# Moving the expert selections of four tiles to the end of their tile, and re-spacing the background work

## The chip, the cores and the metric

The kernel runs on one core of a Trainium2 chip. The metric is the device time of one execution in microseconds (us). Before the change it is 4654.85 us, the median of three runs from 4640.61 to 4658.42 us.

## The reference, cut to what matters

One decoder layer is computed for a prompt of 1024 positions and for 32 sample positions (8 sequences of 4) that share all weights, in float32 with a width of 1024:

```
h   = rmsnorm(x) * (1 + scale1) + shift1
z   = h @ W_in                                  # q, k, v, gMLP u and v, branch gates
A   = differential attention: 8 heads, two softmax maps each, A1 - lambda * A2 weights the values
B   = u * (tril(W_s) v + b) in chunks of 128
x2  = x + gate1 * (sigmoid(gA) * (A @ W_A) + sigmoid(gB) * (B @ W_B)) @ W_o
h2  = rmsnorm(x2) * (1 + scale2) + shift2
s   = (h2 @ W_q) . subkeys                      # 8 heads, two halves of 128 keys
top 16 of each half, top 16 of their 256 sums -> 8 * 16 = 128 experts for each row, softmax gates
y   = x2 + gate2 * sum over experts e of  g_e * gelu(u_e . h2) * v_e
```

The tables u and v have 16384 rows of 1024 float32 (4 KB) each. Every row of the sequence gathers 128 rows of u and 128 rows of v.

## The kernel before, in words

There are three phases: the conditioning products, the projection to z, and the tail, which holds all the rest and which alone the change touches (`tail_phase`). The rows are cut into nine tiles: tiles 0 to 7 are 128 prompt rows each, tile 8 is the 32 sample rows.

The tail starts with a front part (attention of tiles 0 to 3, the mix of tiles 0 and 1, all of the sample's attention, and the selection of tile 0). Then comes the expert loop, one turn for each tile `t`. In turn `t`:

- POOL issues indirect gathers in turn: one brings, for one of the 128 expert slots, a u row for each of the 128 rows of tile `t` (`u_rows`, line 971), the next brings the 128 v rows of one row of tile `t-1` (`v_rows`, line 981). One gather moves 128 rows of 4 KB, or 512 KB. Eight u buffers and eight v buffers are in flight; a gather waits until its buffer was used.
- DVE makes, in program order, one `dot` (line 1877) for each u gather, which waits for that gather. A turn has 128 of them. I call the place of a dot its **slot** `s` (0 to 127). Four slots are a **tick**; a turn has 32 ticks, and the ticks are numbered through: turn 1 begins at tick 32.
- PE adds four v gathers to the result of tile `t-1` in each tick (`add_rows`, line 1307).
- After a dot DVE may do pieces of two other kinds of work. One is the **selection** of tile `t+1`: 81 steps (`select`) that search the scores (MAX8, MATCH_REPLACE8, FIND_INDEX8), build the expert numbers and the gates. The other is the **background**.

The background is a written timetable, `BACK`. It holds the mixes of the pairs of tiles (2,3), (4,5), (6,7) and of the sample (`mix` 1 to 4, 35 steps each: the branch products, x2, h2, and the scores of the selection) and the attention of tiles 4 to 7 (`att` 1, 39 steps). Each entry has steps, a first tick and an end tick, and `timetable` spreads the steps evenly over the ticks; where there are more steps than ticks, two steps share a tick. SP (loads and stores), PE, ACT and DVE each run their part of a step at its tick in their own program order; DVE spreads a step over the four slots of the tick. A mix loads 20 weight blocks of 1 MB through SP's queue: three at its step 0, with the rows of its tiles, one at each of its steps 7 to 14 and 17 to 20, and one at each of its steps 25 to 29, with its part of the sub-keys. In the second entry all attention steps stand ahead of those of mix 2.

A selection can start when the mix that makes its scores is done. There are two places for it. A tile `t` that is not in `LATE` runs the selection of tile `t+1` from slot 36 on, one step after each dot; SP loads its scores at tick 8 of the turn and the h2 rows of the next tile at tick 2. A tile in `LATE` runs it from slot 84 on, two steps after each dot, with the loads at ticks 20 and 21:

```
if t < PT and t not in LATE and S0 <= s < S0 + STEPS:        # S0 = 36, STEPS = 81
    select(t + 1, s - S0)
if t in LATE and S1 <= s:                                    # S1 = 84
    for i in range(2 * (s - S1), min(2 * (s - S1) + 2, STEPS)):
        select(t + 1, i)
for kind, p, k, quarter in AT_SLOT.get(t * P + s, ()) if t < PT else ():
    background[kind](p, k, quarter)
```

ACT's exponential of the gates (`gate_exp`) stands at tick 25, or 29 in a late tile. The first u gather of the next turn waits on POOL for the selection's expert numbers (`s_idx`). After turn 7 the sample's numbers and gates are packed, and its gathers follow.

Of the kernel before, what the change touches and what calls it, by code (L numbers as in the profile page):

```python
# [481 lines left out]
def att_steps(p):  # L482
    return H * len(GROUPS_ATT[p]) + 7
# [6 lines left out]
def every(kind, p):  # L490
    n = {"att": lambda: att_steps(p), "mix": lambda: MIX_STEPS, "satt": lambda: SATT_STEPS}[kind]()
    return [(kind, p, k) for k in range(n)]


def spread(steps, others):

    out, n = [], 0
    for i, step in enumerate(steps):
        out.append(step)
        while n < len(others) and n * len(steps) < (i + 1) * len(others):  # L500
            out.append(others[n])
            n += 1
    return out


def timetable(parts):

    ticks, slots = {}, {}
    for steps, begin, end in parts:
        for i, step in enumerate(steps):  # L510
            ticks.setdefault(begin + i * (end - begin) // len(steps), []).append(step)
    for tick, steps in ticks.items():
        for n in range(TICK * len(steps)):
            slots.setdefault(TICK * tick + n // len(steps), []).append(steps[n // TICK] + (n % TICK,))
    return ticks, slots


def tail_phase(nc, g):
# [22 lines left out]
    KR = 4  # L541
    TPT = P // TICK
    FRONT = spread(every("att", 0) + every("mix", 0), every("satt", 0))
    BACK = ((every("mix", 1), 0, 35),
            (every("att", 1) + every("mix", 2), 35, 116),
            (every("mix", 3), 116, 168),
            (every("mix", 4), 168, 232))
    LATE = (3,)
    AT_TICK, AT_SLOT = timetable(BACK)
    GSTEP = [6, 7, 8, 9, 10, 11, 12, 13, 16, 17, 18, 19] + list(range(24, 32))  # L550

# [44 lines left out]
    place, main, last_in = {}, 0, {}  # L596
    for step in FRONT + [step for steps, _, _ in BACK for step in steps]:
        for key in units(*step):
# [44 lines left out]
    with ExitStack() as ctx:  # L643
# [125 lines left out]
        with nc.Block() as block:  # L769
            @block.sync  # L770
            def _(sp):
# [132 lines left out]
                def load_scores(f):  # L904
                    for b in range(2):
                        sp.wait_ge(s_sst[b], 16 * 4 * min(2 * (f // 2 + 1), TILES))
                    if f > 0:
                        sp.wait_ge(s_idx, f)
                    sp.dma_start(q[0:rows(f), :], g.sc[f * P:f * P + rows(f), :]).then_inc(s_scl, 16)
# [18 lines left out]
                def next_x2(d):  # L928
                    sp.wait_ge(s_st, 16 * (d + 1))
                    if d + 1 < PT:  # L930
                        sp.dma_start(xy[:], g.x2[(d + 1) * P:(d + 2) * P, :]).then_inc(s_x, 16)
                    if d + 1 == PT:
                        for j in range(GP4):
                            m = NS // GP4
                            sp.dma_start(xy[32 * j:32 * j + m, :], g.x2[NP + j * m:NP + (j + 1) * m, :]).then_inc(s_x, 16)
                            for n in range(2):
                                r = 32 * j + n * NDEC
                                sp.dma_start(g2[r:r + NDEC, :],
                                             g.mod[1 + 2 * j + n:2 + 2 * j + n, cols].broadcast_to([NDEC, D])).then_inc(s_g2, 16)
                for t in range(TILES):  # L940
                    for tick in range(TPT if t < PT else 0):
                        for kind, p, k in AT_TICK.get(t * TPT + tick, ()):
                            background[kind](p, k)
                        if tick == (21 if t in LATE else 2) and 1 <= t < PT:
                            sp.wait_ge(s_u, U0[t])
# [3 lines left out]
                        if tick == 6 and t >= 2:  # L949
                            next_x2(t - 2)  # L950
                        if tick == (20 if t in LATE else 8):
                            load_scores(t + 1)
# [373 lines left out]
            def _(act):  # L1326
# [120 lines left out]
                def gate_exp(f):  # L1447
                    r = rows(f)
                    act.wait_ge(s_df, f + 1)
                    nc.scalar.activation(best[0:r], best[0:r], ACT.Exp).then_inc(s_ex, 1)  # L1450

                def gelu(t, c):
                    cols = slice(c * CH, (c + 1) * CH)
                    act.wait_ge(s_u, U0[t] + (c + 1) * CH)
                    nc.scalar.activation(ge[:, cols], a[:, cols], ACT.Gelu).then_inc(s_ge, 1)  # L1455
# [24 lines left out]
                for t in range(TILES + 1):  # L1480
                    for tick in range(TPT):
                        if t in LATE and tick == 29:
                            gate_exp(t + 1)
# [8 lines left out]
                        if t == PT and tick in (18, 31):  # L1492
                            gelu(t, (18, 31).index(tick))
                        if t < PT and t not in LATE and tick == 25:
                            gate_exp(t + 1)

            @block.vector
            def _(dve):
# [344 lines left out]
                def select(f, i):  # L1843

                    if i < 38:
                        (halves_even, halves_odd)[i % 2](f, i // 2)
                    elif i < 40:
                        candidates(f, i - 38)
                    elif i < 62:
                        (sums_even, sums_odd)[i % 2](f, (i - 40) // 2)  # L1850
                    elif i == 62:
                        difference(f)
                    elif i < 65:
                        places(f, i - 63)
                    elif i < 77:
                        pick(f, i - 65)
                    elif i < 79:
                        experts(f, i - 77)
                    elif i < 81:
                        gates(f, i - 79)  # L1860
# [19 lines left out]
                def weights(t, c):  # L1880
                    cols = slice(c * CH, (c + 1) * CH)
                    dve.wait_ge(s_ge, W0[t] + c + 1)
                    if c == 0 and t > 0:
                        dve.wait_ge(s_wt, t)
                    gt = gate[:, t % 2, cols] if t < PT else gate_s[:, cols]
                    if c == 0:
                        dve.wait_ge(s_gate if t < PT else s_pk, t + 1 if t < PT else 2 * QS)
                    nc.vector.tensor_tensor(w[:, cols], ge[:, cols], gt, ALU.mult).then_inc(s_w, 1)
# [19 lines left out]
                for t in range(TILES + 1):  # L1908
                    if t == PT:
                        pack_sample()  # L1910
                    for s in range(NU[t] if t <= PT else 0):
# [5 lines left out]
                        if s % CH == 8 and s > CH:  # L1917
                            weights(t, s // CH - 1)
                        if t < PT and t not in LATE and S0 <= s < S0 + STEPS:
                            select(t + 1, s - S0)  # L1920
                        if t in LATE and S1 <= s:
                            for i in range(2 * (s - S1), min(2 * (s - S1) + 2, STEPS)):
# [13 lines left out]
def build(nc, ins, outs):  # L1936
    g = Shared()
    with ExitStack() as ctx:
# [63 lines left out]
        run(adaln_phase)  # L2002
        run(projection_phase)
        run(tail_phase)


# [61 lines left out]
```

## Time and profile before

| what | value |
|---|---|
| median of three runs | 4654.85 us |
| the profiled execution's own time | 4671.97 us |
| its span, first to last instruction | 4670.3 us |
| busy: PE, DVE, POOL, ACT | 63%, 55%, 57%, 13% |
| DMA | 1550 MB, mean 332 GB/s |
| begin of the expert loop (first dot) | 1497.0 us |
| start of the last dot | 4608.6 us |

The busy shares are means over phases with different limits; the expert loop has to be read by stretches. The rows below cut a turn at slots 0, 36, 84 and 128, which are the places where the selections begin. I call the three stretches the first, middle and last third of a turn, though they have 36, 48 and 44 slots.

### The profile page before, as it was taken

The numbers are of one execution on the slowest core, as the hardware profiler recorded it, in microseconds if no ns is written. First come the engines' busy times: TensorE is split into PE (matmuls) and PEld (weight loads), VectorE is DVE, ScalarE is ACT, GpSimd is POOL, SyncE is SP. The second block draws the span as 40 slices with busy tenths as digits, with TensorE's granted clock in tenths as the row PEclk, the third lists the DMA queues.
The fourth block names the chain that finished last, engine by engine and source line by source line (L and its number), as shares of the span: only waits on it lengthen the run. The fifth ranks groups of instructions, "written<-read, shape, count | busy, mean of one in ns | idle before, by whom it ended". The sixth has DMA issues, their size and how long they took to land.

```text
span 4670.3 us, 46877 instructions
## 1 busy us (share of the span) xinstructions
PE 2941.9 (63%) x16545; PEld 1779.0 (38%) x16545; DVE 2569.1 (55%) x5693; ACT 586.4 (13%) x1207; POOL 2670.9 (57%) x2513
## 2 busy tenths in 40 slices
PE   2899999896882675877365644555534344633354
PEld 1677777564772562434143322322301112300010
DVE  2466633333115896997675448467467556556411
ACT  1111133322111012333000100000000000000000
POOL 2223222233322567877676668667677777777776
PEclk7899999877986786788687776777767665565666
DMA  7322321789974999999999999999999999999999
GB/s 270 123 98 95 125 78 62 251 304 349 351 268 178 368 377 411 383 366 394 419 407 420 419 417 361 408 418 418 412 383 416 405 415 390 400 414 380 352 412 358
DMA packets 468719, 1550.14 MB, mean 332 GB/s; under 512 B 51638, under 2 KB 108407, under 8 KB 453084
## 3 DMA queue, kind: packets, MB, share of 16 engines
q0 software_dynamic: 351376, 1271.99, 69.3%
q1 hardware_dynamic: 116268, 262.92, 14.8%
q10 hardware_dynamic: 864, 12.58, 0.7%
q8 instruction: 113, 1.85, 0.2%
q14 instruction: 98, 0.80, 0.0%
HBM read 1482.18 MB, written 65.23 MB: 331 GB/s over the span
## 4 chain that ended last, share of the span: by engine, by line
POOL 32%; DMA 19%; PE 14%; issue 11%; DVE 5%; POOLq 1%; ACT 0%; SPq 0%; DVEq 0%; ACTq 0%
POOL v_rows L981 16%; POOL u_rows L971 15%; DMA v_rows<-in_peer_v,expertsT 14%; PE ps_y L1307 5%; DMA u_rows<-in_peer_u,experts 3%; PE ps_bank L1166 2%; DVE u_rows L1877 2%; DMA v_rows<-in_cache_v 2%; PE ps_bank L1160 2%; PE ps_bank L1084 1%; PE ps_y L1265 1%; PE ps_bank L1087 1%; POOL u_rows L981 1%; PE ps_y L1224 1%; DMA u_rows<-in_peer_v,expertsT 0%
## 5 line engine op out<-in xcount | busy, mean ns | idle before, releaser
L1877 DVE CUSTOM_DVE_ANT_0 u_rows<-u_rows,h_rows 128x1024 f32<-128x1024 f32 x1056 | 1292.7, 1225 | 1075.5 <-DMA u_rows<-in_peer_u,experts 903.6
L1307 PE MATMUL ps_y<-v_rows,w_columns 128*32 128x512 f32 x4016 | 806.6, 944 | 1310.2 <-DMA v_rows<-in_peer_v,expertsT 1275.4
L971 POOL DMA_INDIRECT u_rows<-in_peer_u,experts x1024 | 1114.0, 1088 | 448.4 <-issue 296.3
L981 POOL DMA_INDIRECT v_rows<-in_peer_v,expertsT x1004 | 1090.9, 1087 | 466.2 <-issue 280.2
L1307 PEld LDWEIGHTS ps_y<-v_rows,w_columns 128*32 128x32 f32 x4016 | 161.7, 147 | 1812.2 <-issue 1810.6
L374 PE MATMUL ps_z<-w_in_high,hT_high 128*128 128x512 f32 (+1 forms) x1008 | 398.9, 396 | 1.5 <-ACTq L383 1.5
L374 PE MATMUL ps_z<-w_in_high,hT_low 128*128 128x512 f32 (+1 forms) x1008 | 397.5, 394 | 0.0
L374 PE MATMUL ps_z<-w_in_low,hT_high 128*128 128x512 f32 (+1 forms) x1008 | 396.1, 393 | 0.0
L349 POOL CAST w_in_high<-w_in_buf 128x4096 fp32r<-128x4096 f32 x13 | 46.8, 3602 | 456.8 <-PE ps_z L374 427.5
L1166 PE MATMUL ps_bank<-turned_a,weights 128*128 128x256 f32 (+1 forms) x1280 | 282.6, 383 | 0.9 <-ACT turned_a L1330 0.9
L1160 PE MATMUL ps_bank<-weights,turned_a 128*128 128x256 f32 (+1 forms) x1152 | 268.9, 394 | 1.8 <-ACT turned_a L1330 1.8
L1166 PEld LDWEIGHTS ps_bank<-turned_a,weights 128*128 128x128 f32 x1280 | 243.8, 213 | 59.7 <-issue 32.9
L1160 PEld LDWEIGHTS ps_bank<-weights,turned_a 128*128 128x128 f32 (+1 forms) x1152 | 215.6, 189 | 75.9 <-issue 37.7
L423 DVE TENSOR_TENSOR z_square<-z_raw 128x512 f32<-128x512 f32 (+1 forms) x54 | 82.4, 1525 | 240.2 <-ACT z_raw L390 235.6
L374 PEld LDWEIGHTS ps_z<-w_in_low,hT_high 128*128 128x128 f32 (+1 forms) x1008 | 181.3, 180 | 53.3
L374 PEld LDWEIGHTS ps_z<-w_in_high,hT_low 128*128 128x128 f32 (+1 forms) x1008 | 180.8, 179 | 54.1
L374 PEld LDWEIGHTS ps_z<-w_in_high,hT_high 128*128 128x128 f32 (+1 forms) x1008 | 180.7, 179 | 53.6 <-ACTq L383 1.7
L1455 ACT ACTIVATE gelu_now<-a_now 128x16 f32<-128x16 f32 x66 | 14.2, 215 | 1352.1 <-DVE a_now L1877 1351.9
L1084 PE MATMUL ps_bank<-kT,qT 64*128 64x512 f32 (+3 forms) x384 | 181.0, 582 | 4.2 <-DVE att_rows L1555 2.5
L1002 POOL DMA_DIRECT2D v_rows<-in_cache_v x128 | 67.9, 531 | 191.9 <-issue 191.0
L995 POOL DMA_DIRECT2D u_rows<-in_cache_kT x128 | 68.2, 532 | 168.9 <-issue 165.9
L1362 ACT ACTIVATE prob<-ps_bank,exp_bias 128x512 f32<-128x512 f32 (+2 forms) x192 | 110.4, 578 | 301.9 <-DVE exp_bias L1523 217.9
(244 smaller groups left out, 3626.8 us busy)
## 6 DMA issues: line engine op xcount, KB each, us to landing
u_rows<-in_cache_kT POOLq DMA_DIRECT2D x128, 512.0 KB, 5.8
v_rows<-in_cache_v POOLq DMA_DIRECT2D x128, 512.0 KB, 6.1
weights<-in_peer_w_q SPq DMA_DIRECT2D x40, 1024.0 KB, 7.7
w_in_buf<-in_w_in POOLq DMA_DIRECT2D x14, 2048.0 KB, 9.4
scratch_z<-z_out SPq DMA_DIRECT2D x112, 256.0 KB, 2.0
weights<-in_w_att_out SPq DMA_DIRECT2D x20, 1024.0 KB, 18.3
weights<-in_w_gm_out SPq DMA_DIRECT2D x20, 1024.0 KB, 8.1
weights<-in_w_out SPq DMA_DIRECT2D x20, 1024.0 KB, 8.1
```

Source lines behind the costliest of these rows:

```text
L374: last = nc.tensor.matmul(ps_z[0:r, n % RING, :], hT[lhs][:, k, t * P:t * P + r], w[rhs][:, b, k, :], start=k == 0 and (lhs, rhs) == (0, 0 ...
L423: link(nc.vector.tensor_tensor(sq[0:r, :], zs[0:r, j, :], zs[0:r, j, :], ALU.mult))
L971: pool.indirect_dma_start(ur[:, slot, :], None, g.peer_u, bass.IndirectOffsetOnAxis(ap=col, axis=0)).then_inc(s_ur[slot], 16)
L981: pool.indirect_dma_start((ur if other else vr)[:, slot, :], None, g.peer_v, bass.IndirectOffsetOnAxis(ap=idxT[:, t % 3, k:k + 1], axis=0) ...
L995: pool.dma_start(skT[:, n % KP, e], g.cache_kT[bass.ds(page, 1)].rearrange("a p h c -> (a p) h c")).then_inc(s_sk[n % KP], 16)
L1002: pool.dma_start(svr[:, n % VP, :], g.cache_vp[bass.ds(page, 1)].rearrange("a p c -> (a p) c")).then_inc(s_svp[n % VP], 16)
L1084: last = nc.tensor.matmul(dst[:, 0:wd], qT[half, par, i * P:(i + 1) * P], kT[half, par, c * CB:c * CB + wd], start=True, stop=not edge)
L1160: last = nc.tensor.matmul(dst[0:r, i * QB:(i + 1) * QB], lT[:, k, i * P:i * P + r], wr[:, slot, k, :], start=k == 0, stop=k == KD - 1)
L1166: last = nc.tensor.matmul(dst[:, jj * QB:jj * QB + n], wr[:, slot, k, jj * P:(jj + 1) * P], A[:, k, 0:n], start=k == 0, stop=k == KD - 1)
L1307: last = nc.tensor.matmul(ps_y[32 * j:32 * (j + 1), b:b + CB], wcol[:, base:base + 32], (ur if four[j][0] else vr)[:, four[j][1], b:b + CB ...
L1362: takes(nc.scalar.activation(prob[:, m, c * CB:c * CB + wd], bank(("s", p, n, m, c))[:, 0:wd], ACT.Exp, bias=nbias[:, b, m:m + 1], scale=S ...
L1877: nc.vector.tensor_tensor_reduce(ur[:, slot, :], ur[:, slot, :], hrow[:, t % 2, :], 1.0, 0.0, ALU.mult, ALU.add, a[:, s:s + 1]).then_inc(s ...
```

## The change

The ticks in the timetable and the set of late tiles change. No instruction is added or removed; the order of the instructions on DVE, PE, ACT and SP does.

```
-    BACK = ((every("mix", 1), 0, 35),
-            (every("att", 1) + every("mix", 2), 35, 116),
-            (every("mix", 3), 116, 168),
-            (every("mix", 4), 168, 232))
-    LATE = (3,)
+    BACK = ((every("mix", 1), 0, 52),
+            (every("att", 1) + every("mix", 2), 52, 116),
+            (every("mix", 3), 116, 180),
+            (every("mix", 4), 180, 244))
+    LATE = (1, 3, 5, 7)
```

In ticks per step: mix 1 goes from 1.00 to 1.49, attention and mix 2 (74 steps) from 1.09 to 0.86, mix 3 from 1.49 to 1.83; mix 4 stays at 1.83 and begins 12 ticks later. Tick 52 is slot 80 of turn 1, tick 116 slot 80 of turn 3, tick 180 slot 80 of turn 5 and tick 244 slot 80 of turn 7.

## Rows read from the trace of the kernel before

**Rows 1.** The page, the span in 40 slices: DMA busy, GB/s.
```profile
DMA  7322321789974999999999999999999999999999
GB/s 270 123 98 95 125 78 62 251 304 349 351 268 178 368 377 411 383 366 394 419 407 420 419 417 361 408 418 418 412 383 416 405 415 390 400 414 380 352 412 358
```

**Rows 2.** The page, chain that ended last, by engine.
```profile
POOL 32%; DMA 19%; PE 14%; issue 11%; DVE 5%; POOLq 1%; ACT 0%; SPq 0%; DVEq 0%; ACTq 0%
```

**Rows 3.** Turns 0, 1, 2, by thirds: us, PE PEld DVE ACT POOL busy, PEclk, DMA share, GB/s.
```profile
1496.96:1569.31 72.35, 40.49 (x179) 34.70 (x178) 55.58 (x102) 6.77 (x13) 49.31 (x40) 0.74 0.95 354
1569.31:1668.52 99.21, 57.98 (x257) 50.08 (x255) 93.59 (x284) 3.04 (x7) 56.30 (x49) 0.80 1.00 399
1668.52:1754.24 85.72, 68.66 (x337) 60.85 (x337) 82.55 (x167) 19.86 (x33) 57.62 (x43) 0.86 0.95 361
1754.24:1861.53 107.29, 60.94 (x242) 23.91 (x246) 62.81 (x122) 21.96 (x58) 83.35 (x75) 0.68 1.04 411
1861.53:2004.04 142.51, 119.19 (x591) 60.11 (x584) 128.48 (x369) 50.35 (x129) 111.83 (x95) 0.82 1.00 380
2004.04:2136.31 132.27, 103.87 (x518) 53.42 (x517) 119.41 (x271) 44.15 (x117) 103.04 (x88) 0.83 1.00 378
2136.31:2239.66 103.35, 71.22 (x375) 37.03 (x377) 74.09 (x149) 31.92 (x79) 80.41 (x73) 0.83 1.01 396
2239.66:2383.48 143.82, 60.74 (x330) 27.26 (x326) 96.41 (x274) 11.49 (x21) 102.16 (x97) 0.69 1.02 409
2383.48:2523.97 140.49, 95.70 (x467) 59.54 (x458) 88.10 (x184) 5.70 (x10) 97.13 (x91) 0.82 1.02 420
```

**Rows 4.** Turn 3, middle and last third; turn 4, middle; the same columns.
```profile
2632.61:2788.24 155.63, 91.97 (x488) 57.75 (x483) 59.55 (x99) 12.91 (x23) 97.31 (x95) 0.77 1.03 418
2788.24:2926.88 138.64, 67.52 (x349) 34.18 (x341) 116.95 (x338) 9.54 (x17) 111.20 (x91) 0.73 0.96 370
3036.89:3181.52 144.63, 71.06 (x344) 35.12 (x339) 94.35 (x270) 8.25 (x16) 101.97 (x97) 0.68 1.02 417
```

**Rows 5.** Turn 5 and turn 7, by thirds; the same columns.
```profile
3311.32:3418.32 107.00, 43.89 (x224) 20.45 (x227) 46.81 (x78) 6.08 (x12) 73.34 (x70) 0.69 1.03 412
3418.32:3552.82 134.50, 52.94 (x267) 15.24 (x263) 91.50 (x261) 3.42 (x10) 105.28 (x96) 0.66 0.99 384
3552.82:3680.34 127.52, 59.43 (x281) 19.04 (x273) 83.66 (x169) 3.52 (x6) 97.15 (x91) 0.72 1.02 419
4051.01:4148.88 97.87, 37.69 (x176) 13.57 (x179) 47.02 (x77) 1.94 (x8) 72.59 (x72) 0.57 1.02 397
4148.88:4275.00 126.12, 42.90 (x200) 8.25 (x195) 85.32 (x248) 0.87 (x4) 97.41 (x95) 0.62 1.01 397
4275.00:4405.36 130.36, 41.94 (x189) 7.93 (x181) 81.25 (x169) 3.52 (x6) 93.75 (x88) 0.59 0.93 352
```

**Rows 6.** Turn 7 from slot 124 to the first dot of turn 8; the same columns.
```profile
4385.12:4405.36 20.24, 6.39 (x29) 1.10 (x21) 6.07 (x18) 0.22 (x1) 8.02 (x8) 0.58 0.55 200
```

**Rows 7.** DVE groups, turn 1's last third: busy, mean ns, idle before, releaser.
```profile
L1877 DVE CUSTOM_DVE_ANT_0 u_rows<-u_rows,h_rows 128x1024 f32<-128x1024 f32 x44 | 53.6, 1219 | 2.0 <-DMA u_rows<-in_peer_u,experts 2.0
L1546 DVE SCALAR_TENSOR_TENSOR diff_prob<-prob,map_coef 128x1024 f32<-128x1024 f32 (+3 forms) x10 | 10.9, 1090 | 4.8 <-PE ps_bank L1096 4.5
```

**Rows 8.** DVE groups, turn 3's middle third.
```profile
L1877 DVE CUSTOM_DVE_ANT_0 u_rows<-u_rows,h_rows 128x1024 f32<-128x1024 f32 x48 | 58.9, 1227 | 96.0 <-DMA u_rows<-in_peer_u,experts 96.0
```

**Rows 9.** DVE groups, turn 3's last third: mix 3's first and last.
```profile
L1596 DVE SCALAR_TENSOR_TENSOR u_then_b<-ps_bank,gate_bias,u_then_b 128x128 f32<-128x128 f32 x16 | 4.4, 329 | 0.0
...
L1578 DVE RECIPROCAL head_rstd<-head_std 128x8 f32<-128x8 f32 x2 | 0.4, 184 | 0.0
```

**Rows 10.** POOL groups, turn 3's middle third.
```profile
L971 POOL DMA_INDIRECT u_rows<-in_peer_u,experts x48 | 49.1, 1023 | 14.6 <-issue 14.6
```

**Rows 11.** POOL groups, turn 3's last third.
```profile
L971 POOL DMA_INDIRECT u_rows<-in_peer_u,experts x46 | 58.7, 1276 | 14.0 <-issue 14.0
```

**Rows 12.** DMA issues: count, KB each, median us to landing.
```profile
weights<-in_w_att_out SPq DMA_DIRECT2D x20, 1024.0 KB, 18.3
```

## The prediction, made before the change was run

> **What bounds the kernel now.** I read the page's slices first. From slice 14 on the 16 DMA engines are busy over 90% at mostly 360 to 420 GB/s [rows 1], so the expert loop, two thirds of the span, lives by its gathers. The chain of waits agrees: POOL, which issues them, has 32%, DMA 19%, PE 14%, DVE 5% [rows 2]. Then I cut the loop at the slots where selections begin, in the view of windows [rows 3 to 5]. The reader is to see three kinds of stretch. (1) Those at 418 to 420 GB/s with a DMA share over 1.02: the DMA engines are the limit, and DVE waits for u rows (96 of 156 us in turn 3's middle third [rows 8]). I take 418 GB/s as the full rate. (2) Those in which DVE is nearly solid: turn 0's middle and last (93.6 of 99.2, 82.6 of 85.7) and turn 1's (128.5 of 142.5, 119.4 of 132.3), where a dot waits 2 us in all for its row [rows 7] and the rate is 361 to 399. (3) Turn 3's last third, where the kernel already has a late selection: DVE 117 of 139 us, 370 GB/s [rows 4], gathers of 1276 ns each on POOL [rows 11] against 1023 in the third before [rows 10].
>
> Bytes follow as time x rate: turn 3's last third moved 138.64 x 0.370 = 51.3 MB, which at 418 takes 122.7 us. So a late selection loses 16 us in its third. A selection in its ordinary place loses too: turn 5's middle third moved 51.6 MB in 134.5 us where 123.6 would do (11 us), turn 7's 50.1 MB in 126.1 (6 us) [rows 5].
>
> **The change, turn by turn.** No instruction comes or goes, so each turn is what is bound there after the move. A weight block is 1.05 MB [rows 12]; with its other loads and stores I count 34 MB for a prompt mix, 22 for the sample's, 1.6 for a head of attention. Against 418 GB/s, 1 MB is 2.4 us.
>
> *Turn 0.* Mix 1 had 32 of its steps here, now 22 (the last is step 21): 9.6 MB leave, and on DVE little (the h2 pair, some 5 us). DVE was busy 55.6 + 93.6 + 82.6 = 231.7 of 257.3 us [rows 3]. If DVE becomes the only limit, 231.7 - 5 and a first load of about 9 us leave 236 (-22); if the 25.6 us of waits stay, -4. The waits lie mostly in the first third, whose loads at mix step 0 don't move. I take -14.
>
> *Turn 1, slots 0 to 84.* The selection goes and attention goes, mix 1's steps 22 to 34 come. Before, 107.3 x 0.411 + 142.5 x 0.380 = 98.3 MB in 249.8 us. Now 84 pairs of gathers (88.1) + 10.1 of mix 1 + 2.6 of the first two heads + 0.5 = 101.3 MB, DVE nearly free: 242 us at 418. -8 (0 if the rate stays where it is, -15 if fewer loads fall before slot 84).
>
> *Turn 1, slots 84 to 128.* Here the whole selection (two steps a slot) meets attention, now at 1.16 steps a tick where it was 0.91. Selection and 44 dots cost what turn 3's last third shows without mix 3: 117 less 13.8 (six DVE groups, the first and last in [rows 9]) = 103 us. An attention step costs DVE between 3.8 and 5.2 us: the third held ten of them before, as its ten rows of L1546 show [rows 7], and the same third of turn 7, which has none, was busy 81.3 us; 119.4 - 81.3 gives 3.8 of work, 132.3 - 81.3 gives 5.1 with waits for PE (middle third: (142.5 - 85.3)/11 = 5.2). Now steps 2 to 13 run here, 11 full ones: 42 to 57 us. Sum 145 to 160, against 132.3 before. DVE has no slack in this third, so I am nearer the upper end: 160, +28 (bounds +13 and +33, the latter with 12 full steps).
>
> *Turn 2.* Attention's last step is at slots 80 to 83 instead of 48 to 51. DVE in the first third 74 + 2.4 steps x 3.8 = 83 of 103 us, in the middle 96 - 11 (mix 2's beginning goes) + 12 x 3.8 = 131 of 144: it fits, but only just. Bytes -0.9 MB. I take +3 (-5 to +20; the upper end is rival D's).
>
> *Turns 3, 4, 6: bytes alone.* Mix 2 brings 5.8 MB more into turn 3 ahead of slot 84, at 418 (+14), mix 3 2 MB less behind it, where DVE is the limit (-1). Turn 4 loses 4.9 MB at 417 (-12), turn 6 gets 1.5 (+4). Together +5 (-5 to +10).
>
> *Turn 5.* Slots 0 to 84: 95.7 MB before; mix 3's end brings 7.0, mix 4's beginning is as large as before, the loads at ticks 2 and 8 (1.5 MB) go behind slot 84. 101 MB at 418 is 242 us, against 241.5: the selection's 11 us pay for the bytes. Last third: like turn 3's, with a mix half as large: 130, against 127.5. +3. Bounds: -12 if the late third runs at 418 (47.4 MB, 113 us), +11 if it is turn 3's 138.6.
>
> *Turn 7.* The same way: 89 + 5.9 - 1.5 = 93.4 MB, 223 us against 224. Last third: 130.4 before, of which 20 us are the drain behind slot 124, when POOL has no numbers for the sample's rows yet [rows 6]. Now 125.6 (turn 3's slots 84 to 124) - 13 + 20 + 3 for a selection that ends seven slots later: 136. +6 (-9 to +14).
>
> *Waits.* POOL's first u gather of the next turn waits for the expert numbers, which come after dot 123 instead of 114; queued behind it are v gathers, and PE waits for those. By then POOL has seven u rows issued ahead, and turn 3 shows this end already: it is in its 138.6. SP's score load moves from tick 8 to 20, one tick ahead of its reader as now, behind the q, k and v loads of two heads in turn 1.
>
> Sum: -14 - 8 + 28 + 3 + 5 + 3 + 6 = **+23 us**. The profiled execution took 4671.97 (span 4670.3 and 1.7 around it): 4695. That execution lies 17 above the median of the runs, 4654.85; a difference carries over, so 4678.
>
> On what dense DVE work does to the gathers: the row is POOL's 1276 ns a gather in the late third against 1023 [rows 10, 11]. The Trainium skill (SBUF — State Buffer, section "Who interferes with whom") says that only copies, casts and scalar operations in their two-port modes keep GpSimd from writing descriptors, and that searches, reductions and two-tensor operations don't; the selection is nearly all of the latter. By that rule the late third would run at the full rate; this trace has it at 370, with the cause open. The rule would put turns 5 and 7 at their lower ends; its result is rival B.
>
> **The rivals.** *B: it comes out even.* The late third is slow in turn 3 by accident of its place, DVE's 105 us lie beside gathers at 418, and turns 5 and 7 give -12 and -9 instead of +3 and +6: +23 - 30 = -7, and with turn 1's third at 150, not 160, it is -17 at the least. For it: DVE has 20 us to spare in that third [rows 4]. Against: POOL is without a pause there, and its gathers are longer. Time 4648 (4638, or 4663 if of the two only turn 5 gains).
>
> *C: faster.* One mechanism: DVE's work, not the bytes, costs the rate. Then every stretch that loses its selection runs at 418 and turn 0 gains all its waits: -22 - 15, and the jam in turn 1 costs only the work, +13, because the waits for PE (5 us in ten steps [rows 7]) vanish in longer ticks; turns 5 and 7 -12 and -9, the rest +8: -37, 4618. It decides from the point where turn 1's last third stays under 145 us and turn 5's middle third reaches 418. Against: DVE was without slack in that third already.
>
> *D: clearly slower.* Attention at 1.16 steps a tick fills PE. In turn 1's middle third PE was busy 119.2 of 142.5 us for 11 steps; turn 7's, with the additions alone, 42.9. So a step costs 6.9 us and a tick's additions 3.6; 6.9 x 1.16 + 3.6 + the idle time as it was (1.9) = 13.5 us a tick, where it was 11.9: over 21 ticks of turn 2 +34, less my 3: +54, 4709. Against: the granted clock (a mean over its two levels, 1.2 and 2.4 GHz) was 0.82 to 0.86 of 2.4 GHz in the stretches in which PE was busiest, 0.57 to 0.69 in idle ones [rows 3, 5], so a fuller PE is a faster one.
>
> That the timetable binds nothing is excluded: DVE and PE run their steps in program order between the dots and the additions.
>
> **How the numbers follow.** A measurement tells some 0.5% (23 us) from no change. Chances: forecast 0.42, B 0.26, C 0.16, D 0.16. The forecast's own bounds (-10 to +50, not all ends at once) put half of it above +23 and the rest within. Slower: 0.21 + 0.16 + a little = 0.40; same: 0.20 + 0.22 = 0.42; faster: C and the low end of B, 0.18. The likeliest case gives 4678; range 4630 to 4728, which cuts off half of C and the far end of D. The likeliest case alone: 4645 to 4705.
>
> **What would show it.** Right: turn 0 near 243 us; turn 1's slots 84 to 128 at 155 to 165 with DVE solid and POOL waiting for DVE's dots, which it doesn't do there now; the first two thirds of turns 1, 5 and 7 at 410 GB/s or more; late thirds of turns 5 and 7 under 390. Wrong: turn 1's last third under 145 or turn 2 over 400 with PE solid; gathers of the late thirds near 1023 ns.

## The result, and the profile after

The changed kernel takes 4722.06 us (median of five, 4713.91 to 4724.69), against 4654.85: a ratio of 1.0153, 95% interval 1.0134 to 1.0171. It is slower by 67 us; the forecast was +23. The profiled execution took 4724.01 us with a span of 4722.2.

First the page of the changed kernel: two lines of the span in 40 slices, and the chain that ended last by engine (they answer to [rows 1, 2]).

```profile
DMA  7323221789866999999999999999999999999899
GB/s 278 114 95 112 107 75 64 258 328 371 335 228 234 364 356 418 412 328 351 365 397 420 419 418 353 418 419 403 406 413 372 388 408 411 363 417 410 324 420 359
...
POOL 29%; DMA 20%; PE 14%; issue 11%; DVE 8%; POOLq 1%; ACT 0%; SPq 0%; DVEq 0%; ACTq 0%
```

The largest falls against [rows 1] are in slices 18 to 20 (turn 1's late third and most of turn 2's first two: 328, 351 and 365 for 366, 394 and 419), in 31 and 38, which hold the late thirds of turns 5 and 7 (372 and 324 for 416 and 352), and in 35, the end of turn 6 (363 for 400). Slice 25, turn 3's late third, has 353 and was low before too (361). DVE's share of the chain grew from 5% to 8%.

Next the windows of the changed kernel, cut at the same slots as [rows 3 to 5] and with the same columns: turns 0, 1 and 2 by thirds, turn 3's middle and last third, turn 4's middle, turns 5 and 7 by thirds.

```profile
1483.77:1554.02 70.25, 33.81 (x151) 29.13 (x152) 53.92 (x98) 7.09 (x13) 52.68 (x40) 0.71 0.95 355
1554.02:1647.51 93.49, 34.58 (x139) 28.82 (x137) 89.11 (x275) 0.65 (x3) 64.84 (x50) 0.69 0.95 359
1647.51:1735.88 88.37, 32.01 (x145) 27.69 (x145) 86.13 (x183) 11.26 (x18) 53.66 (x43) 0.67 0.90 331
1735.88:1839.97 104.09, 59.01 (x294) 34.87 (x295) 45.65 (x76) 6.16 (x14) 75.66 (x73) 0.73 1.02 413
1839.97:1980.69 140.72, 76.24 (x398) 40.70 (x400) 61.48 (x105) 11.49 (x25) 104.73 (x99) 0.73 1.03 414
1980.69:2140.62 159.93, 128.67 (x554) 65.49 (x547) 152.72 (x438) 48.82 (x133) 101.03 (x87) 0.78 0.89 326
2140.62:2254.97 114.35, 99.82 (x521) 56.29 (x523) 92.41 (x199) 51.01 (x130) 81.49 (x74) 0.88 0.99 382
2254.97:2401.97 147.00, 97.97 (x533) 52.39 (x529) 119.13 (x345) 39.00 (x102) 115.71 (x98) 0.82 0.98 369
2401.97:2542.52 140.55, 87.78 (x443) 53.51 (x436) 94.84 (x197) 12.00 (x19) 97.43 (x89) 0.78 1.01 410
...
2662.53:2822.09 159.56, 99.77 (x528) 66.53 (x524) 59.47 (x100) 15.68 (x28) 99.26 (x96) 0.79 1.03 419
2822.09:2961.65 139.56, 54.52 (x287) 22.28 (x280) 116.06 (x334) 9.54 (x17) 111.81 (x91) 0.66 0.95 363
...
3065.10:3205.64 140.54, 75.44 (x384) 40.30 (x376) 92.23 (x268) 3.00 (x8) 99.70 (x99) 0.75 1.03 420
...
3332.59:3443.60 111.01, 58.06 (x297) 35.09 (x301) 46.90 (x77) 5.33 (x12) 80.37 (x74) 0.75 1.02 406
3443.60:3579.97 136.37, 64.17 (x324) 30.12 (x320) 59.50 (x99) 7.40 (x14) 94.93 (x94) 0.70 1.03 412
3579.97:3717.34 137.37, 51.94 (x239) 14.44 (x232) 110.87 (x322) 6.21 (x12) 109.95 (x91) 0.56 0.95 353
...
4093.27:4200.65 107.38, 49.10 (x281) 24.31 (x285) 46.97 (x77) 3.15 (x12) 75.94 (x75) 0.62 1.02 411
4200.65:4326.47 125.82, 63.85 (x311) 29.05 (x305) 59.53 (x99) 3.14 (x12) 94.74 (x95) 0.54 1.03 408
4326.47:4460.42 133.95, 41.65 (x189) 7.84 (x181) 106.64 (x317) 3.52 (x6) 97.97 (x86) 0.61 0.90 341
```

By turns, from first dot to first dot (traces; us):

| turn | before | after | difference | forecast |
|---|---|---|---|---|
| 0 | 257.3 | 252.1 | -5 | -14 |
| 1, slots 0 to 84 | 249.8 | 244.8 | -5 | -8 |
| 1, slots 84 to 128 | 132.3 | 159.9 | +28 | +28 |
| 2 | 387.7 | 401.9 | +14 | +3 |
| 3, 4 and 6 | 402.9, 384.4, 370.7 | 419.1, 370.9, 375.9 | +16, -14, +5 | +13, -12, +4 |
| 5 | 369.0 | 384.8 | +16 | +3 |
| 7 | 354.3 | 367.2 | +13 | +6 |

The loop is 68 us longer by these two traces. Their front parts, which are the same code, differ by 13 us the other way (loop begins at 1497.0 and 1483.8 us). And the trace of before was itself long in turn 7: three other executions of that turn's unchanged code (first_half, denser_att and more_dve_before, below) took 341 us. So turn 7 lost some 26 us, not 13; that trace lay 17 us above the median.

The groups of POOL in the changed kernel, late thirds of turns 1, 3 and 5 in that order; the last columns are the idle time ahead of the group and what ended it (turn 3's pair answers to [rows 11]):

```profile
L981 POOL DMA_INDIRECT v_rows<-in_peer_v,expertsT x43 | 52.6, 1224 | 36.1 <-PE ps_y L1307 25.1 <-issue 11.0
L971 POOL DMA_INDIRECT u_rows<-in_peer_u,experts x44 | 49.5, 1124 | 23.1 <-issue 13.1 <-DVE experts L1829 10.0
...
L981 POOL DMA_INDIRECT v_rows<-in_peer_v,expertsT x45 | 57.4, 1275 | 14.0 <-issue 13.4 <-PE ps_y L1307 0.6
L971 POOL DMA_INDIRECT u_rows<-in_peer_u,experts x46 | 54.7, 1189 | 14.0 <-issue 14.0
...
L971 POOL DMA_INDIRECT u_rows<-in_peer_u,experts x45 | 55.5, 1233 | 13.7 <-issue 13.7
L981 POOL DMA_INDIRECT v_rows<-in_peer_v,expertsT x46 | 54.9, 1194 | 14.0 <-issue 13.7 <-PE ps_y L1307 0.3
```

In turns 3 and 5 POOL has no wait worth naming: its busy time and the pause of 0.30 us behind each gather fill the third (110.0 + 27.4 of 137.4 us in turn 5). POOL is the limit there, because a gather takes 1.2 us instead of 0.95. In turn 1 POOL waits, for PE's additions (25 us) and for the selection's expert numbers (10 us); DVE is busy 152.7 of 159.9 us, so I take it as the limit there.

Why are gathers long? The timeline of the changed kernel, turn 3's last third, shows it: columns are start, duration, engine, line and operation. First POOL, then DVE around the same gathers.

```profile
2833.86 1.89 POOL L981 DMA_INDIRECT v_rows<-in_peer_v,expertsT  x1 [0.31 <-issue]
2836.05 0.94 POOL L971 DMA_INDIRECT u_rows<-in_peer_u,experts  x1 [0.30 <-issue]
...
2857.46 3.02 POOL L971 DMA_INDIRECT u_rows<-in_peer_u,experts  x1 [0.30 <-issue]
```

```profile
2833.71 1.21 DVE L1877 CUSTOM_DVE_ANT_0 u_rows<-u_rows,h_rows 128x1024 f32<-128x1024 f32 x1
...
2835.91 0.28 DVE L1736 FIND_INDEX8 half_top_i<-half_top,scores_rest 128x8 uint32<-128x128 f32 x1
...
2857.33 1.20 DVE L1587 TENSOR_TENSOR mixed<-mixed,subln_gain 128x1024 f32<-128x1024 f32 x1
2858.45 1.21 DVE L1877 CUSTOM_DVE_ANT_0 u_rows<-u_rows,h_rows 128x1024 f32<-128x1024 f32 x1
```

The first gather starts 0.15 us into a dot and ends 0.83 us after the dot's end (2834.92). The second starts beside a search and takes 0.94 us. The third starts in a two-tensor product with a dot right behind it, and ends 0.82 us after the end of both (2859.66). The longer a dot has still to run, the longer the gather: in the trace of before, gathers that start 1.1 to 1.2 us ahead of a dot's end take 1.98 us on average, 0.5 to 0.6 us ahead 1.37, under 0.1 us ahead 0.947. Over the whole of that trace, 474 of 475 gathers longer than 1.05 us started while DVE ran a dot, a TENSOR_TENSOR or a SCALAR_TENSOR_TENSOR, and the median end was 0.82 us after that operation's end. The 860 that started while DVE was idle took 0.947 us on average; so did the ones beside TENSOR_REDUCE (0.947) and MAX8 (0.948). I call a gather longer than 1.05 us a **held** gather.

### The profile page after: what moved, and what is told of

Same layout as the page of the kernel before. It is cut to its first block, busy times and chain, and to the rows that moved or that the text cites. A ratio compares the mean times of both kernels' runs of the same rounds, so it can differ in the third digit from the quotient of the medians.

```text
span 4722.2 us, 46871 instructions
## 1 busy us (share of the span) xinstructions
PE 2923.1 (62%) x16545; PEld 1768.8 (37%) x16545; DVE 2567.2 (54%) x5693; ACT 577.8 (12%) x1201; POOL 2694.4 (57%) x2513
## 4 chain that ended last, share of the span: by engine, by line
POOL 29%; DMA 20%; PE 14%; issue 11%; DVE 8%; POOLq 1%; ACT 0%; SPq 0%; DVEq 0%; ACTq 0%
POOL v_rows L981 15%; DMA v_rows<-in_peer_v,expertsT 14%; POOL u_rows L971 13%; PE ps_y L1307 5%; DVE u_rows L1877 3%; DMA u_rows<-in_peer_u,experts 2%; DMA v_rows<-in_cache_v 2%; PE ps_bank L1160 2%; PE ps_bank L1166 2%; DMA u_rows<-in_peer_v,expertsT 1%; PE ps_bank L1084 1%; POOL u_rows L981 1%; PE ps_y L1265 1%; DVE neg_max L1517 1%; PE ps_bank L1087 1%
## 5 line engine op out<-in xcount | busy, mean ns | idle before, releaser
L1307 PE MATMUL ps_y<-v_rows,w_columns 128*32 128x512 f32 x4016 | 791.9, 928 | 1295.1 <-DMA v_rows<-in_peer_v,expertsT 1261.6
L981 POOL DMA_INDIRECT v_rows<-in_peer_v,expertsT x1004 | 1111.0, 1107 | 509.1 <-issue 282.2
```

The costliest lines, as they stand in the source:

```text
L981: pool.indirect_dma_start((ur if other else vr)[:, slot, :], None, g.peer_v, bass.IndirectOffsetOnAxis(ap=idxT[:, t % 3, k:k + 1], axis=0) ...
L1307: last = nc.tensor.matmul(ps_y[32 * j:32 * (j + 1), b:b + CB], wcol[:, base:base + 32], (ur if four[j][0] else vr)[:, four[j][1], b:b + CB ...
```

## The experiments

**1. The two halves of the change.** *first_half* has the new ticks of mix 1, attention and mix 2 and `LATE = (1, 3)`; *second_half* the new ticks of mixes 3 and 4 and `LATE = (3, 5, 7)`.

```
first_half                                          second_half
+ BACK = ((every("mix", 1), 0, 52),                   BACK = ((every("mix", 1), 0, 35),
+         (every("att", 1) + every("mix", 2), 52, 116),       (every("att", 1) + every("mix", 2), 35, 116),
          (every("mix", 3), 116, 168),              +         (every("mix", 3), 116, 180),
          (every("mix", 4), 168, 232))              +         (every("mix", 4), 180, 244))
+ LATE = (1, 3)                                     + LATE = (3, 5, 7)
```

> The timetable and the late places of turns 0 to 3 alone (mix 1 in ticks 0 to 52, attention and mix 2 in 52 to 116, late selections in turns 1 and 3); mixes 3 and 4 as before. Theory 1 (each turn pays for its own crowding, no interplay): the turns 0 to 3 of the changed kernel gave -5, +23, +14, +16 by its trace; without mix 3's smaller share turn 3 keeps +14, so +46 us. Theory 2 (the loss is a slower state of the whole loop, from a phase between engines that any new order can bring): it doesn't split, a half has nearly all of the +67 or nearly none.

> Mixes 3 and 4 at the new ticks (116 to 180, 180 to 244) with late selections in turns 3, 5 and 7; turns 0 to 2 as before. Theory 1: turn 3 -3, turn 4 -13, turn 5 +16, turn 6 +5, turn 7 +13, so +18 us, and with the first half's it makes the whole +67 within 10. My forecast's terms for the same turns: -12 +3 +4 +6 = about 0. Theory 2: as for the first half.

Measured: 1.0091 (1.0073 to 1.0110) and 1.0050 (1.0032 to 1.0068). The sum, 1.41%, is the whole within its interval, and the turns nearly agree one by one: first_half has turns 1 and 2 at 406.9 and 402.4 us (404.7 and 401.9 in the changed kernel), second_half turns 5 and 7 at 380.0 and 367.8 (384.8 and 367.2). So theory 1 holds: the effects add up turn by turn, and each half is slower by itself.

**2. Places without ticks, ticks without places.** *places* has only the new `LATE`; *denser_att* has attention and mix 2 at ticks 52 to 116 and nothing else.

```
places:      - LATE = (3,)                                     + LATE = (1, 3, 5, 7)
denser_att:  - (every("att", 1) + every("mix", 2), 35, 116)    + (every("att", 1) + every("mix", 2), 52, 116)
```

> The old timetable with late selections in turns 1, 3, 5 and 7: only the place of three selections changes. If the late place itself costs (gathers are held up where the selection is dense): turn 1 late third 142 to 155 us (103 of dots and selection, ten attention steps of 3.8 to 5.1) with its middle third 10 to 15 faster, turn 5 and turn 7 late thirds +8 to +12 and +4 to +8, middle thirds -6 and -4 at most: +5 to +25 us. If the place costs nothing and the moved bytes and the denser attention do it all: 0 within 8 us, turns 5 and 7 unchanged.

> Mix 1 in ticks 0 to 35 and the late set as before, attention and mix 2 pushed together into ticks 52 to 116, nothing from 35 to 52. If the jam of selection and attention in turn 1 is what costs in the first half, it goes with the ordinary selection: turn 1's last third has 81 us of dots and half a selection and 11 to 12.7 steps of 3.8 to 5.1 us, 125 to 145 against 160 in the changed kernel; turn 2 keeps its +11 to +14 if it is the denser attention and turn 3 its +14 of bytes: in all +15 to +30 us. If denser attention alone is the cost: turn 1's last third 155 or more, in all +40.

Measured: 1.0024 (1.0010 to 1.0037) and 1.0018 (1.0002 to 1.0033). Three windows: turn 1's last third in places, the same in denser_att, and turn 2's first third in denser_att.

```profile
1985.39:2134.99 149.60, 116.09 (x532) 58.81 (x525) 144.54 (x421) 43.13 (x114) 103.73 (x89) 0.78 0.93 342
```

```profile
1960.89:2100.51 139.62, 110.24 (x537) 55.99 (x537) 127.60 (x291) 52.33 (x140) 105.56 (x91) 0.85 0.99 365
2100.51:2212.84 112.33, 99.03 (x525) 55.77 (x527) 92.29 (x198) 48.56 (x124) 81.44 (x72) 0.89 0.99 387
```

Turn 1's jam is about the sum of both edits: the selection alone makes its last third 149.6 us (+17), denser attention alone 139.6 (+7), both 159.9 (+28). Turn 2's first third is 112.3 with denser attention alone and 101.0 in places: that loss is attention's. In places the thirds that lost their selection became shorter (turn 5's middle 131.6, turn 1's 135.7), those that got it longer (turn 7's last 141.2). The thirds of denser_att came out as expected, its total did not: 0.18% is 8 us, not the 15 to 30, because turn 1's middle third, which attention has left, fell from 142.5 to 123.6 us. So denser attention alone costs hardly anything in all, though it costs turn 2 13 us and turn 3, to which bytes of mix 2 move, 15.

**3. The held gathers, taken away.** *psum_before* is the kernel before in which, in turns 3 to 7 and the sample's, the dots read the row of h2 from two PSUM banks, to which ACT copies it at the head of the turn; mixes 2 to 4 make do with three banks, their gate products spread over two steps. *psum_after* is the changed kernel with the same edit.

```
+ ps_h2 = ctx.enter_context(nc.psum_tensor("ps_h2_rows", [P, D], F32))      # instead of two of the five banks
+ nc.scalar.activation(ps_h2[:], hrow[:, t % 2, :], ACT.Copy).then_inc(s_hp, 1)       # ACT, tick 0, t >= 3
- tensor_tensor_reduce(ur[:, slot, :], ur[:, slot, :], hrow[:, t % 2, :], ...)
+ tensor_tensor_reduce(ur[:, slot, :], ur[:, slot, :], ps_h2[:] if t >= 3 else hrow[:, t % 2, :], ...)
```

> The kernel before, but in turns 3 to 8 the dots read the h2 rows from two PSUM banks (ACT copies them there at the head of the turn; mixes 2 to 4 use three banks for their products instead of five), so a dot has one input in SBUF. Theory L (a gather that starts while DVE runs an instruction with two inputs in SBUF is held until that instruction ends, and in turns 3 to 7 this sets POOL's pace): no gather is held by a dot, the mean falls from 1.03 to 1.28 us to under 1.0, turn 3's last third from 139 to 120 to 128, turns 3 to 7 together by 30 to 60 us, the whole 0.987 to 0.994 of before. Theory J (DVE's own work is what costs in the late thirds): DVE works as long as before, turn 3's last third stays at 135 to 140 and the time within 0.3%.

> The changed kernel with the same edit for turns 3 to 8. Theory L: the late thirds of turns 5 and 7 lose what the change had put on them, 137 and 134 to 118 to 126, and the difference to the edited kernel before shrinks from 67 us to the first half's part, 35 to 50. Theory J: late thirds at 130 or more, the difference stays 60 to 70.

Measured: **0.9911** (0.9894 to 0.9927; 4607.30 us, faster than both kernels) and 1.0035 (1.0013 to 1.0056). Turn 3's last third and its POOL groups in psum_before, to be held against [rows 4, 11]:

```profile
2776.55:2901.17 124.62, 70.87 (x349) 35.47 (x341) 115.33 (x337) 10.78 (x18) 89.38 (x90) 0.75 1.02 413
...
L992 POOL DMA_INDIRECT v_rows<-in_peer_v,expertsT x45 | 46.7, 1037 | 19.6 <-issue 11.6 <-PE ps_y L1320 8.0
L982 POOL DMA_INDIRECT u_rows<-in_peer_u,experts x45 | 43.6, 968 | 15.7 <-issue 11.0 <-DVE a_now L1903 2.4 <-DVE experts L1851 2.3
```

DVE does the same work (115.3 us busy, 117.0 before), the gathers are shorter (8 of 90 held, 29 of 90 before), the rate is 413 instead of 370 GB/s, and the third is 14 us shorter. Late thirds of turns 3, 5 and 7 in psum_after: 122.4, 122.1 and 123.5, against 139.6, 137.4 and 134.0. So the late thirds were slow by held gathers. But the change still costs 60 us in this pair (4667.26 against 4607.30), not the 35 to 50 expected: the dots in PSUM help both kernels, each where its selections lie, and in turns 3 to 7 held gathers explain little of what the change costs. By turns: 35 of the 58 that the traces differ are turns 1 and 2, which have no PSUM dots, and much of the rest is in stretches like turn 5's middle third, here in psum_after, where no gather is held, and then in psum_before:

```profile
3429.45:3565.54 136.09, 62.97 (x328) 29.70 (x324) 59.27 (x99) 7.40 (x14) 87.72 (x93) 0.73 1.03 415
...
3391.58:3517.16 125.58, 52.01 (x268) 14.98 (x263) 90.57 (x261) 3.40 (x10) 93.79 (x98) 0.66 1.03 417
```

In psum_after DVE is idle more than half of it and the DMA share is 1.03: 136.1 us, as the changed kernel's 136.4, where psum_before takes 125.6. This is the bytes of the moved mix: SP's transfers there are 6.2 MB for 1.6, and 4.6 MB at 415 GB/s are 11 us.

**4. The same in every turn.** *psum_all* is psum_before with the PSUM dots from turn 0 on, so that attention and mix 1 also have three banks.

```
- PSUM_FROM = 3        + PSUM_FROM = 0
```

> The kernel before's timetable, with the row of h2 that the dots read copied to two PSUM banks by ACT in every turn from 0 on, so that all background work (mixes 1 to 4 and attention) has three banks instead of five. With the same edit from turn 3 on, 0.9911 was measured. Theory L (a gather that starts in an operation with two SBUF operands is held to 820 ns after its end): turns 1 and 2 lose their held gathers as well; but DVE, not POOL, is the limit in turn 1, so at most 10 us more are gained there, and turn 0's DVE-bound stretches stay. Against it stand three banks for attention and mix 1: if PE's products wait for banks, turn 1's middle and last thirds get longer than 142 and 132 us. I expect turns 0 to 2 within -15 to +25 us of before's, and a ratio of 0.988 to 0.997.

Measured: 0.9965 (0.9943 to 0.9986), 4626.67 us: within the expected range, and slower than psum_before. Turn 1's middle third takes 156.3 us, its last 144.1 (142.5 and 132.3 before). PE's first group in that middle third:

```profile
L1095 PE MATMUL ps_bank<-kT,qT 64*128 64x512 f32 (+3 forms) x88 | 44.1, 605 | 23.9 <-ACT prob L1375 20.4 <-DVE att_rows L1578 3.5
```

PE waits 24 us for a bank that ACT and DVE still read; before, its score products waited 3.4 us there. The third has 9 held gathers of 97, where it had 41 of 94, and still takes 14 us longer: there two banks are worth more than the holds.

**5. Work between the dots.** *two_inputs* is the changed kernel with 40 added TENSOR_TENSORs behind dots 40 to 79 of turn 7, whose middle third now has no selection.

```
+ if t == 7 and 40 <= s < 80:
+     nc.vector.tensor_tensor(yg[:, 0:CB], hrow[:, 1, 0:CB], hrow[:, 1, CB:D], ALU.add).then_inc(s_extra, 1)
```

> The changed kernel with 40 added DVE instructions, one after each of the dots 40 to 79 of turn 7, where DVE has no other work: an addition of two inputs in SBUF, 128x512, about 0.68 us. Theory L: gathers that start in it are held; held gathers (over 1.05 us) in the middle third go from 8 of 94 to 25 or more and the third from 126 us to 132 to 145. Theory J: DVE has 2.6 us a slot and uses 1.25, so nothing: 124 to 129, held ones as before.

Measured in one execution: the third takes 124.5 us (125.8 without), and the gathers are no longer than in the changed kernel. POOL's groups there:

```profile
L982 POOL DMA_INDIRECT v_rows<-in_peer_v,expertsT x48 | 49.2, 1025 | 16.4 <-issue 14.0 <-PE ps_y L1308 2.4
L972 POOL DMA_INDIRECT u_rows<-in_peer_u,experts x47 | 45.9, 976 | 14.3 <-issue 14.3
```

Theory L's expectation missed, the rival's came out: 8 of 94 gathers are held, as without the added work. A gather and its pause take 0.945 + 0.305 = 1.25 us, hardly more than a dot, and in this stretch two gathers pass for each dot. Of the 94, 44 start some 0.1 us before a dot's end and 46 start 1.1 to 1.3 us after one, when the added operation (0.70 us) is over, so the 28 us of added operations fall where hardly any gather starts. So more two-input work alone need not hold gathers. That the selection holds them because its steps of uneven length shift the dots against the gathers is argued, not shown: no run varies it alone.

**6. What sets turn 2's first third (103 to 114 us)?** *no_mask* is the changed kernel that leaves out the causal mask on the diagonal blocks of tiles 4 to 7, and so a part of the computation; that saves PE work alone. *more_dve_after* and *more_dve_before* add 16 one-input reductions (0.68 us) behind every second dot of slots 5 to 35 of turn 2. *adds_first* lets PE do a tick's additions ahead of attention in turn 2.

```
no_mask:     - edge = c == rounds(t) - 1         + edge = c == rounds(t) - 1 and p == 0
more_dve_*:  + if t == 2 and s < 36 and s % 2 == 1 and s > 4:
             +     nc.vector.tensor_reduce(yg[:, 0:1], hrow[:, 0, 0:CB], AX.X, ALU.max).then_inc(s_extra, 1)
adds_first:  + in turn 2, tick % 8 != 0: add_rows(t - 1, tick * GP4), then background[kind](p, k)
```

> The changed kernel without the causal mask on the diagonal blocks of tiles 4 to 7 (64 matrix products of 0.33 us less on PE in the attention of turns 1 and 2, 22 groups of them in turn 2's first third): part of the computation is left out. If PE sets turn 2's first third (POOL waited 12 us there for PE's additions, 2 before): 114 us falls by 6 to 11, to 103 to 108. If DVE does: within 2 us of 114. Turn 1's last third, which I hold to be DVE's, stays at 157 to 161 in both.

> The changed kernel with 16 added reductions of 128x512 from one SBUF operand (about 0.7 us each, 11 us in all), one behind every second dot of turn 2's slots 5 to 35. Theory V (DVE's own work and the waits inside attention's chain set turn 2's first third, 114.35 us in the changed kernel): the third becomes 7 to 11 us longer, 121 to 125. Rival (bytes or gathers set it): at most 3 us longer.

> The same 16 reductions in the kernel before, where the third took 103.35 us and DVE waited for u rows. Theory V: the added work goes into those waits, and the third becomes 0 to 4 us longer. If it becomes 7 to 11 us longer here too, DVE was the limit already, and the comparison with the changed kernel says nothing of what the change did.

> The changed kernel; in turn 2 alone PE runs a tick's additions of v rows ahead of its attention step, not behind it (ticks 0, 8, 16 and 24 keep the order). In turn 2's first third (114.35 us in the changed kernel, 103.35 before) POOL waited 12.1 us for additions that stood behind attention in PE's order, where it waited 2.0 before. Theory W (that order costs the third): POOL's wait for the additions falls under 4 us, and the third takes 103 to 109 us. Rival (the 11 us are DVE's: its attention work and the waits for PE inside it): POOL's wait falls, but the third stays at 112 to 118 us, and DVE waits longer for PE.

Measured in one execution each; where its code is that of the changed kernel, this third took 112.6 to 114.4 us in four traces, and where it is that of before 101.0 to 103.4 in four, so 2 us more or less say little. The third in no_mask, more_dve_after, more_dve_before and adds_first, in this order, and in adds_first also the DVE group that waits longest for PE inside attention (line 1546 in the changed kernel):

```profile
2137.65:2251.02 113.37, 81.28 (x470) 46.53 (x472) 92.47 (x199) 51.15 (x131) 83.15 (x75) 0.83 0.99 380
```

```profile
2147.14:2263.77 116.63, 102.77 (x525) 55.70 (x523) 101.41 (x214) 50.98 (x130) 87.63 (x74) 0.88 0.99 382
```

```profile
2138.20:2240.76 102.56, 68.53 (x375) 36.55 (x377) 83.12 (x165) 32.09 (x79) 79.94 (x71) 0.82 1.01 398
```

```profile
2127.39:2255.61 128.22, 100.96 (x521) 55.51 (x523) 92.14 (x198) 50.98 (x130) 81.26 (x75) 0.85 0.97 366
...
L1549 DVE SCALAR_TENSOR_TENSOR diff_prob<-prob,map_coef 128x640 f32<-128x640 f32 (+3 forms) x11 | 11.7, 1066 | 29.0 <-PE ps_bank L1096 28.8
```

PE's work is not the limit: 18 us less of it gave 1 us. DVE's work alone is not: 11 us more cost 2.3, since the waits for rows (5.7 to 1.5 us) and for PE shrank; my theory V missed. Nor are held gathers: all gathers of the third together kept POOL busy for 80.4 us before [rows 3] and 81.5 after. The place of the additions is not what costs either: put first they made the third 14 us longer, for PE's part of attention then came late and DVE waited 28.8 us for it, where it waits 9.8 in the changed kernel. The wait of POOL for additions hardly fell (9.7 us of 12.1), so both expectations missed. Of these edits the third reacts most to the one that delays PE's products inside an attention step. That denser attention causes the loss is shown (experiment 2); which hand-over in the ring of DVE, PE and POOL ends last is not settled.

## Why the prediction was right in sign and wrong in size

*In short.* The sign, the place of the jam and turns 3, 4 and 6 were right. The steps that failed are sizes of terms: turn 2 ("it fits, but only just", +3, measured +14), turn 5's late third ("like turn 3's, with a mix half as large", +2.5, measured +10), "418 GB/s as the full rate" (406 to 414 in the first two thirds of turns 1, 5 and 7), the loads that were to go behind slot 84 (they did not), and the waits of turn 0 that were to go in part (-14, measured -5). The measured time lies inside the range, 4630 to 4728, but outside the bounds of the forecast alone, 4645 to 4705; only rival D, whose mechanism fails, had put the range so high. That it holds the result is luck.

*What held.* DVE as the limit of turn 1's last third: 160 us forecast, 159.9 measured, with DVE busy for 152.7 of them. It jams about as the sum of experiment 2 says. That the number is exact is luck: I had 11 attention steps at 5.2 us, and the trace has 12 rows of L1546, which makes (159.9 - 103) / 12 = 4.7 for each. One detail was wrong: POOL waits there for PE's additions and for the expert numbers, not for dots, so the wait for numbers that I saw only inside turn 3's 138.6 us does come out in turn 1 (10 us). Turns 3, 4 and 6 by bytes alone: +16, -14, +5 against +13, -12, +4. Late thirds of turns 5 and 7 under 390 GB/s: 353 and 341. Turn 1 up to slot 84 moved the 101.2 MB that I had counted, but at 413 GB/s, not 418: -5, not -8.

*Turn 0: -5, not -14.* The term lay midway between "If DVE becomes the only limit" (-22) and "if the 25.6 us of waits stay" (-4), and the waits stayed: DVE was busy 229.2 us after, 2.5 less than before, and idle 23 us still. SP moved 9.3 MB less in turn 0 (my count was 9.6), and what followed was mostly a lower rate, 359 and 331 GB/s for 399 and 361 in its last two thirds: the bytes left a place where DVE is the limit, and came to turns where DMA is.

*Turn 2: +14, not +3.* "It fits, but only just" compared DVE's busy time, 83 of 103 us in the first third, with the length. The 83 was itself too small: "2.4 steps x 3.8" took every attention step before as a full one, but the last of them only drain what earlier ones began. The DVE rows of this third, before and after, show four steps more, not 2.4:

```profile
L1546 DVE SCALAR_TENSOR_TENSOR diff_prob<-prob,map_coef 128x768 f32<-128x768 f32 (+3 forms) x7 | 7.8, 1114 | 7.1 <-PE ps_bank L1096 7.0
...
L1546 DVE SCALAR_TENSOR_TENSOR diff_prob<-prob,map_coef 128x640 f32<-128x640 f32 (+3 forms) x11 | 11.7, 1066 | 10.0 <-PE ps_bank L1096 9.8
```

DVE's work became 92.4 us and the third 114.4: of 18 us of added work, 7 went into idle time and 11 lengthened the third, though 22 us of idle time were left. Work outside the chain fits into that time (experiment 6: 11 us cost 2.3); more steps of the chain from PE to DVE to PE did not. The other two thirds gave +3. My bound of +20 came from rival D, whose mechanism (PE filled) experiment 6 refutes: PE was busy 285.6 of turn 2's 401.9 us, and less PE work changed hardly anything.

*Turn 5: +16, not +3.* Two terms. "130, against 127.5" in the late third scaled turn 3's loss by the size of the mix; measured were 137.4. The mix was not the cause: POOL's gathers are held as in turn 3 (1233 and 1194 ns), and without the holds the third takes 122.1 (experiment 3). My own bound of 138.6 had it. And "101 MB at 418" was right in bytes (111.0 x 0.406 + 136.4 x 0.412 = 101.3 MB) but ran at 409: 247, not 242. Turn 5's first third was at 412 already before [rows 5], so the rate stood in the rows and I took the best one.

*Turn 7: +13 by the traces, some +26 against ordinary executions of the old turn.* Its late third was right (134.0 for 136). The first two thirds took 233.2 us for 223: 95.5 MB, where I had 93.4, at 410 GB/s. I had sent the loads of scores and h2 (1.5 MB) behind slot 84: they stand at ticks 20 and 21, from slot 80 on, but in the trace SP issues them at slots 60 and 61 (in turn 5 at slot 62), and the sample's are only 0.8 MB. Some 1.5 MB more of gathers fell into the stretch as well. The moved mix makes this: with only the places changed the first third took 95.4 us, with mixes 3 and 4 moved 108.4. The +6 was also measured against a profile whose turn 7 was 13 us too long: I compared stretches of one execution as if each were typical, and its 17 us above the median were a warning.

Those terms add up: +9 in turn 0, +3 in turn 1, +11 in turn 2, +3 in turns 3, 4 and 6, +13 in turn 5, +7 in turn 7 are, but for rounding, the 45 us between the 68 of the traces and my 23.

*The rivals.* B rested on a rule for held gathers, and fell: moving a selection late costs the rate in turns 5 and 7 too. I had read the Trainium skill (SBUF — State Buffer, section "Who interferes with whom") as saying that two-tensor operations leave GpSimd alone. The section says in full that a DVE instruction with two SBUF inputs contends with a GpSimd instruction that reads SBUF, and infers, for the writing of descriptors, that it needs the write interface, which a two-tensor operation does not take. The indirect gathers here, whose row numbers lie in SBUF, are held by such instructions, 474 of 475 long ones; with the dots' operand in PSUM the kernel takes 0.9911. That agrees with the rule for an instruction that reads SBUF. No run here separates the reading of row numbers from the writing of descriptors, so whether the inference fails stays open; my step from it to these gathers did fail. C fell as turn 1's last third came out over 145; D's cause is wrong, and its place, turn 2, lost 14 us where D had 34. That its total, 4709, is nearer than mine is luck.

## What to carry to other kernels

Before a stage is moved, ask for each stretch whether its bytes or its DVE time bind: bytes taken from a stretch that DVE binds come back at full price in one that DMA binds. Two background works that share an engine cost about their sum where it has no slack, and a chain that passes between engines needs more room than its busy time. Count the steps of a pipeline from their rows in the trace, not from the timetable: its last steps do less. Where indirect gathers run beside two-input DVE work, look at the duration of single gathers first; putting the operand that all the dots share into PSUM was worth more here (0.9%) than any change of the timetable tried, all of which were slower. In turn 1, where attention needed the two banks, it cost 21 us (experiment 4 against 3).

## What the runs showed of the hardware

- An indirect gather of 128 rows of 4 KB occupies POOL for 0.945 us, with 0.30 us behind it. One that starts while DVE runs an operation with two SBUF operands mostly ends 0.82 us after that operation, or after a later one where several follow at once (7.54 us the longest, at the end of the changed kernel's turn 6).
- Of 377 gathers that started beside a search or a one-input reduction of DVE in the traces of before and after, 2 were long.
- With the dots' second operand in PSUM (psum_before), 0 to 6 of the 70 to 97 gathers of a third were long in turns 4 to 7, and a dot took 1204 ns in turn 3's last third, where [rows 7, 8] have 1219 and 1227.
- In turn 7's middle third, with two gathers of 1.25 us for each dot, 90 of 94 gathers started at the same two places behind a dot, and 28 us of added two-input work there changed nothing.
- Stretches of the changed kernel with a DMA share of 1.02 or 1.03 ran at 406 to 420 GB/s: one figure for the full rate was too sharp.
